# Entry of x: rows scaled before the turn, the turn made with the identity, six PSUM banks, two engines emptying them

## The chip, the cores and the metric

The kernel runs on one core of one Trainium2 chip. The metric is the device time of one execution in microseconds (us). The engines are TensorE (PE in the rows), VectorE (DVE), ScalarE (ACT), GpSimd (POOL) and SyncE (SP), which here only issues transfers.

## The reference, cut to what matters

One layer of a hybrid network on 512 tokens of width 2048. Everything begins with a normalised x that is multiplied by a wide weight matrix:

```python
def rms_norm(x, g):
    xf = x.astype(jnp.float32)
    y = xf * lax.rsqrt(jnp.mean(xf * xf, axis=-1, keepdims=True) + NORM_EPS)
    return (y * g.astype(jnp.float32)).astype(x.dtype)

h = rms_norm(x, norm_mix[l])
proj = h @ w_in[l]
u_s5, x_lru, g_lru, p_rw, z_ssd, xbc_ssd, dt_ssd = _split(proj, [...])
```

Four mixers (an S5 scan, an RG-LRU, an RWKV-7 recurrence, an SSD block) then work on the columns of `proj`, an output projection adds to x, and a mixture of 64 experts follows, then a last norm.

## The kernel before, in words

All data are fp32. The program is one stream of instructions for each engine, in an order written out by hand, with semaphores between them.

**The entry**, which the change touches, goes from x in memory to `hT`, the normalised x with its 2048 channels on the partitions (16 chunks of 128 channels, 512 tokens wide). The tokens come in four tiles `i` of 128 rows (`NTT` is 4), `xs[:, i, :]` of 128x2048.

- SyncE loads the four tiles (L515), then the first slab of w_in (L528), then 18 small parameter tables (L508), then the second slab of w_in.
- ScalarE loads six small tables, then squares each tile and sums its rows (L898), and takes the root of the mean (L900), which it tells by `rs_ok`. Behind the fourth tile its queue issues the S5 tables and others (L901 to L918), and only then comes its first exponential for the S5 parameters (L928).
- VectorE inverts the root (L1212), 128x1, and writes a diagonal matrix from it: the identity times the factor, 128x128 (`rdiag`, L1214, told by `setup_ok`).
- TensorE first turns the table with the norm's gains (L2079; VectorE copies it to `colB`, L1218), then makes one ordinary matmul for every 128x128 block of x against the diagonal (L2088). That turns the block and scales it at once. Four blocks `j` fill one PSUM bank; bank number `m` runs over 16 groups, group `m` being tile `m // 4` and channel chunks `4 * (m % 4)` on. Four banks (2 to 5) are used in turn, so group m waits until group m - 4 has been emptied (`tr_used`).
- VectorE empties every group with one product with the gains, 128x512 (L1226).
- TensorE then begins the projection (L2284): 38 column tiles `n`, each 16 matmuls of 128x128 by 128x512. An ordinary fp32 matmul stands as two MATMUL records in the trace, a transpose as one. Behind column tile 0 it turns the S5 tables (L2093, L2096), for which they must have landed. ScalarE copies each column tile to SBUF (L925).

GpSimd meanwhile zeroes buffers (L671 to L687, the last two of 128x2048 for the S5 matrices), writes the ones of the identity (L689, told by `mask_ok`) and builds masks (L692 to L717).

## Time and profile before

| | |
|---|---|
| median of 3 runs | 2533.95 us (2529.70, 2533.95, 2533.98) |
| profiled execution, its own time | 2538.04 us |
| its span | 2535.9 us |
| mean granted TensorE clock | 0.968 |
| entry: first block of x turned | 10.34 us |
| entry: last group emptied | 28.17 us |
| projection begins | 27.28 us |

The span is what the hardware profiler covers of one execution; some 2 us of the execution's own time lie outside it. All times in the rows below count from the start of the span.

### The profile page before, as it was taken

How to read it: one execution, taken by the hardware profiler on the slowest of the kernel's cores; microseconds unless marked ns; L12 is line 12 of the kernel's file. 1: busy time of each engine (PE TensorE's matmuls, PEld its weight loads, DVE VectorE, ACT ScalarE, POOL GpSimd, SP SyncE). 2: the span in 40 equal slices, each digit the busy share in tenths (PEclk: the TensorE clock that was granted, in tenths of full speed). 3: DMA queues.
4: the chain of work that ended last, by engine and by line, in shares of the span. 5: the costliest groups of instructions: out<-in, count | busy, mean ns of one | idle time of the engine just before them, and what ended most of it. 6: DMA issues, size and time to landing. Idle time of an engine off the chain costs nothing.

```text
span 2535.9 us, 32657 instructions
## 1 busy us (share of the span) xinstructions
PE 2327.9 (92%) x12979; PEld 1218.8 (48%) x12979; DVE 836.9 (33%) x1324; ACT 351.8 (14%) x596; POOL 395.5 (16%) x577
## 2 busy tenths in 40 slices
PE   8999999999899999999998988988888988888886
PEld 5443444455588876644443444444443444344442
DVE  5499937434644432411111111111111111111114
ACT  2100023201422222110000000000000000000002
POOL 3366400000042200011111101111011111111110
PEclk9999999999999999999999999999999999999998
DMA  6221221221122145599999999999999999999998
GB/s 190 69 81 33 67 66 55 67 66 61 42 93 71 49 155 212 220 400 424 426 425 427 425 425 426 426 427 424 426 426 428 426 425 426 427 427 424 425 426 332
DMA packets 143251, 714.61 MB, mean 282 GB/s; under 512 B 33768, under 2 KB 92972, under 8 KB 99788
## 3 DMA queue, kind: packets, MB, share of 16 engines
q1 hardware_dynamic: 115688, 691.09, 66.6%
q0 software_dynamic: 18432, 16.83, 1.9%
q10 hardware_dynamic: 9060, 5.68, 0.8%
q8 instruction: 53, 0.87, 0.1%
q14 instruction: 18, 0.15, 0.0%
HBM read 718.11 MB, written 45.61 MB: 301 GB/s over the span
## 4 chain that ended last, share of the span: by engine, by line
PE 43%; DMA 42%; DVE 11%; issue 2%; ACT 1%; POOL 0%; SPq 0%; DVEq 0%; ACTq 0%; POOLq 0%
DMA big<-in_moe_w 41%; PE ps L2284 12%; PE ps L2631 11%; PE ps L2338 5%; DVE big L1246 4%; PE ps L2660 3%; PE ps L2508 2%; PE ps L2428 1%; DVE big L1378 1%; DVE big L1377 1%; PE ps L2413 1%; PE ps L2645 1%; DMA big<-y_rows 1%; DVE big L1415 1%; PE ps L2088 1%
## 5 line engine op out<-in xcount | busy, mean ns | idle before, releaser
L2631 PE MATMUL ps<-big 128*64 128x384 f32 x4096 | 697.2, 495 | 103.6 <-DMA big<-in_moe_w 90.8
L2631 PEld LDWEIGHTS ps<-big 128*64 128x64 f32 x4096 | 298.5, 139 | 509.2 <-issue 369.9
L2284 PE MATMUL ps<-big 128*128 128x512 f32 (+1 forms) x1184 | 519.1, 598 | 1.6 <-ACT big L946 1.6
L2660 PE MATMUL ps<-big 128*64 128x512 f32 x1536 | 388.8, 661 | 51.7 <-DVE big L2023 51.7
L2284 PEld LDWEIGHTS ps<-big 128*128 128x128 f32 (+1 forms) x1184 | 224.3, 191 | 287.2 <-issue 285.1
L2019 DVE TENSOR_SCALAR big<-ps,scal 128x384 f32<-128x384 f32 x64 | 39.5, 618 | 698.8 <-PE ps L2631 698.8
L2660 PEld LDWEIGHTS ps<-big 128*64 128x64 f32 x1536 | 115.1, 150 | 277.9 <-issue 217.3
L2030 DVE SCALAR_TENSOR_TENSOR big<-ps,scal,big 128x512 f32<-128x512 f32 x128 | 90.2, 747 | 388.6 <-PE ps L2660 388.6
L2338 PE MATMUL ps<-big 128*128 128x256 f32 x768 | 184.8, 391 | 3.6 <-DMA big<-in_w_out 2.5
L2338 PEld LDWEIGHTS ps<-big 128*128 128x128 f32 x768 | 142.3, 192 | 28.7 <-issue 4.8
L846 POOL COPY scal<-slots 128x3 f32 (+1 forms) x64 | 11.9, 186 | 906.8 <-DVE big L2030 888.8
L1180 ACT ACTIVATE big<-ps,scal 128x384 f32<-128x384 f32 x64 | 37.1, 580 | 798.5 <-PE ps L2631 769.4
L2645 PE MATMUL ps<-stacked,big 128*128 128x64 f32 x768 | 141.2, 334 | 0.8 <-issue 0.8
L2645 PEld LDWEIGHTS ps<-stacked,big 128*128 128x128 f32 x768 | 138.8, 261 | 1.4 <-issue 1.4
L1246 DVE TENSOR_TENSOR big<-big 128x512 f32<-128x512 f32 (+7 forms) x129 | 110.8, 880 | 47.1 <-ACT big L953 40.0
L1185 ACT ACTIVATE big<-ps 128x192 f32<-128x192 f32 x64 | 21.1, 330 | 522.4 <-PE ps L2645 522.4
L1945 DVE TENSOR_TENSOR big<-ps,gffn 128x512 f32<-128x512 f32 x128 | 82.5, 686 | 0.5
L925 ACT ACTIVATE big<-ps 128x512 f32<-128x512 f32 (+2 forms) x38 | 22.5, 594 | 431.8 <-PE ps L2284 431.8
L2615 PEld LDWEIGHTS ps<-ident,big 128*128 128x128 f32 x512 | 62.0, 194 | 38.6 <-issue 38.6
L2615 PE MATMUL ps<-ident,big 128*128 128x128 f32 x512 | 74.1, 288 | 0.8 <-DMA big<-x_rows,idxg 0.8
L842 POOL DMA_INDIRECT big<-x_rows,gix x62 | 64.7, 1043 | 55.6 <-POOL gix L838 52.0
L857 POOL DMA_INDIRECT y_rows<-big,six x63 | 64.1, 1018 | 55.7 <-POOL six L854 55.7
(412 smaller groups left out, 1701.5 us busy)
## 6 DMA issues: line engine op xcount, KB each, us to landing
big<-in_moe_w SPq DMA_DIRECT2D x191, 3072.0 KB, 38.6
big<-in_w_in SPq DMA_DIRECT2D x18, 2048.0 KB, 8.4
big<-in_w_out SPq DMA_DIRECT2D x8, 1024.0 KB, 6.0
big<-y_rows SPq DMA_DIRECT2D x8, 1024.0 KB, 11.8
big<-in_x SPq DMA_DIRECT2D x4, 1024.0 KB, 8.4
big<-in_w_out SPq DMA_DIRECT2D x8, 512.0 KB, 7.5
big<-in_x SPq DMA_DIRECT2D x16, 256.0 KB, 2.8
big<-in_w_out SPq DMA_DIRECT2D x1, 4096.0 KB, 15.8
```

Of the source, the lines that this page charges most:

```text
L842: nc.gpsimd.indirect_dma_start(xg[k], None, x2g, bass.IndirectOffsetOnAxis(ap=of, axis=0), bounds_check=T * GR - 1, oob_is_err=False).then ...
L857: nc.gpsimd.indirect_dma_start(ydg, bass.IndirectOffsetOnAxis(ap=six[k][:, 0:1], axis=0), yb[k], None, bounds_check=2 * T * GR - 1, oob_is ...
L1246: v.do(nc.vector.tensor_tensor(out, a, b, o))
L1945: nc.vector.tensor_tensor(xT[k][:, cs, :].rearrange("p c (g t) -> p c g t", g=GR), ps[h][:, 0:NJ * P // 2].rearrange("p (c g t) -> p c g t ...
L2030: nc.vector.scalar_tensor_tensor(out=yb[k][:, cs], in0=ps[5 + q][:], scalar=scal[k][:, 0:1], in1=yb[k][:, cs], op0=MUL, op1=ADD).then_inc( ...
L2284: last = nc.tensor.matmul(ps[n % 2][0:wd, :], ring[s % 2][:, k, c:c + wd], hT[:, k, :], start=(k == 0), stop=(k == NC - 1))
L2338: last = nc.tensor.matmul(ps[b][:, 256 * i:256 * i + 256], ready[c][:, P * (2 * h + i):P * (2 * h + i) + P], w, start=(j == 0), stop=(j == ...
L2508: last = nc.tensor.matmul(o[:], V_[:, q, P * i:P * i + P], wo_rw[:, q, 512 * ncol:512 * ncol + 512], start=(q == 0), stop=(q == WT - 1))
L2615: last = nc.tensor.transpose(ps[h][:, P * j:P * j + P], xg[k].rearrange("t (p c) -> t c p", c=NJ)[:, c], ident[:])
L2631: last = nc.tensor.matmul(ps[2 + w][B * g:B * g + B, 0:FF], xT[k][:, j, B * g:B * g + B], W13[k][w][:, NJ * g + j, :], start=(j == 0), sto ...
L2645: last = nc.tensor.matmul(o, uv[k][:, w, :].rearrange("p (t c) -> p c t", c=FC)[:, m], stacked[:], start=True, stop=True)
L2660: last = nc.tensor.matmul(ps[5 + q][B * g:B * g + B, :], hid[k][:, m, :], W2[k][:, m, 512 * n:512 * n + 512], start=(m == 0), stop=(m == F ...
```

## The change

The rows of x are scaled before they are turned. For tiles 0, 1 and 2 GpSimd multiplies the 128x2048 tile in place by the factor that VectorE has inverted (told by `xsc_ok`), tile 3 is multiplied by VectorE itself. TensorE then turns the blocks in transpose mode with the plain identity. The groups use six banks in turn (2, 3, 4, 5, 7, 1) in place of four. VectorE empties the groups of tiles 0, 1 and 3; those of tile 2 (m = 8 to 11) are emptied by ScalarE, with one 128x128 copy with a scale for each block, sixteen in all, told by `tr_used_act`. The identity is finished before the large memsets on GpSimd; the last large memset (`Gin[1]`) comes behind the three multiplications.

```diff
-        rdiag = big[:, 76, :]
...
+        xsc_ok = sem("xsc_ok")
+        XBANK = (2, 3, 4, 5, 7, 1)
...
             nc.gpsimd.memset(prmB, 0.0).then_inc(zero_ok, 1)
+            g.settle()
+            nc.gpsimd.affine_select(out=ident[:], in_=ident[:], compare_op=ALU.not_equal, fill=1.0, base=0,
+                                    pattern=[[-1, P]], channel_multiplier=1).then_inc(mask_ok, 1)
...
             nc.gpsimd.memset(Gin[0], 0.0)
+
+            for i in range(NTT - 1):
+                pool.wait_ge(setup_ok, i + 1)
+                nc.gpsimd.tensor_scalar(xs[:, i, :], xs[:, i, :], st[:, 8 + i:9 + i], None, ALU.mult).then_inc(xsc_ok, 1)
             nc.gpsimd.memset(Gin[1], 0.0).then_inc(gin_zero, 1)
-            pool.wait_ge(gin_zero, 1)
-            nc.gpsimd.affine_select(out=ident[:], in_=ident[:], compare_op=ALU.not_equal, fill=1.0, base=0,
-                                    pattern=[[-1, P]], channel_multiplier=1).then_inc(mask_ok, 1)
+            pool.wait_ge(gin_zero, GIN_ZERO + 1)
...
                 nc.scalar.activation(st[:, 4 + i:5 + i], st[:, i:i + 1], ACT.Sqrt, bias=epsb[:], scale=1.0 / D).then_inc(rs_ok, 1)
+            act.wait_ge(prm_col, 1)
+            for c4 in range(4):
+                m = 4 * (NTT - 2) + c4
+                act.wait_ge(tr_ok, m + 1)
+                for j in range(4):
+                    c = 4 * c4 + j
+                    g0 = PB["norm_mix"][0] + c
+                    last = nc.scalar.activation(hT[:, c, P * (NTT - 2):P * (NTT - 1)], ps[XBANK[m % 6]][:, P * j:P * j + P], ACT.Copy,
+                                                scale=colB[:, g0:g0 + 1])
+                last.then_inc(tr_used_act, 1)
...
-            def rms_diag(i):
+            def rms_factor(i):
                 dve.wait_ge(rs_ok, i + 1)
-                v.do(nc.vector.reciprocal(st[:, 8 + i:9 + i], st[:, 4 + i:5 + i]))
-                v.settle()
-                v.tell(nc.vector.tensor_scalar(rdiag[:, P * i:P * i + P], ident[:], st[:, 8 + i:9 + i], None, ALU.mult), setup_ok, i + 1)
-
-            rms_diag(0)
+                ins = nc.vector.reciprocal(st[:, 8 + i:9 + i], st[:, 4 + i:5 + i])
+                if i < NTT - 1:
+                    v.tell(ins, setup_ok, i + 1)
+                else:
+                    v.do(ins)
+                    v.settle()
+                    v.tell(nc.vector.tensor_scalar(xs[:, i, :], xs[:, i, :], st[:, 8 + i:9 + i], None, ALU.mult), setup_ok, i + 1)
+
+            rms_factor(0)
...
+            rms_factor(1)
-            for m in range(NTT * 4):
+            for m in [m for m in range(NTT * 4) if m // 4 != NTT - 2]:
                 i, c4 = divmod(m, 4)
-                if c4 == 2 and i + 1 < NTT:
-                    rms_diag(i + 1)
+                if c4 == 2 and i < 2:
+                    rms_factor(i + 2)
...
                 if c4 == 0:
-                    pe.wait_ge(setup_ok, i + 1)
-                if m >= 4:
-                    pe.wait_ge(tr_used, m - 3)
+                    if i < NTT - 1:
+                        pe.wait_ge(xsc_ok, i + 1)
+                    else:
+                        pe.wait_ge(setup_ok, i + 1)
+                if m >= 6:
+                    turned_out(m - 6)
                 for j in range(4):
                     c = 4 * c4 + j
-                    last = nc.tensor.matmul(ps[2 + m % 4][:, P * j:P * (j + 1)], xs[:, i, P * c:P * (c + 1)], rdiag[:, P * i:P * i + P],
-                                            start=True, stop=True)
+                    last = nc.tensor.transpose(ps[XBANK[m % 6]][:, P * j:P * (j + 1)], xs[:, i, P * c:P * (c + 1)], ident[:])
...
                     if n == 0 and k % 4 == 0:
-                        pe.wait_ge(tr_used, NTT * 4 - 3 + k // 4)
+                        for i in (NTT - 2, NTT - 1):
+                            turned_out(4 * i + k // 4)
```

`turned_out(m)` waits on TensorE until group m has been emptied, by ScalarE's count for tile 2 and by VectorE's for the others.

On VectorE, at the start of its stream, the order before (`st` holds the norm factors, `ps` is a PSUM bank, `big` is SBUF: the diagonal in the row with `ident`, `hT` in the rows with `colB`):

```order
L1212 RECIPROCAL st<-st 128x1
L1214 TENSOR_SCALAR big<-ident,st 128x128
L1218 COPY colB<-ps 128x128
L1226 TENSOR_TENSOR big<-ps,colB 128x4x128 x2
L1212 RECIPROCAL st<-st 128x1
L1214 TENSOR_SCALAR big<-ident,st 128x128
L1226 TENSOR_TENSOR big<-ps,colB 128x4x128 x4
L1212 RECIPROCAL st<-st 128x1
L1214 TENSOR_SCALAR big<-ident,st 128x128
L1226 TENSOR_TENSOR big<-ps,colB 128x4x128 x4
L1212 RECIPROCAL st<-st 128x1
L1214 TENSOR_SCALAR big<-ident,st 128x128
```

and of the change (the row `big<-big,st` is the multiplication of tile 3 in place):

```order
L1228 RECIPROCAL st<-st 128x1
L1238 COPY colB<-ps 128x128
L1228 RECIPROCAL st<-st 128x1
L1247 TENSOR_TENSOR big<-ps,colB 128x4x128 x2
L1228 RECIPROCAL st<-st 128x1
L1247 TENSOR_TENSOR big<-ps,colB 128x4x128 x4
L1228 RECIPROCAL st<-st 128x1
L1234 TENSOR_SCALAR big<-big,st 128x2048
L1247 TENSOR_TENSOR big<-ps,colB 128x4x128 x6
```

The four small diagonals are gone, one multiplication of 128x2048 stands between the emptying of m = 5 and m = 6, and 12 groups are left of 16.

On GpSimd, from the small memsets on, before (`big` is the parameter tables, then the LRU, S5 and the two `Gin` buffers):

```order
L679 MEMSET big 128x1024
L680 MEMSET eps 128x1
L681 ISA
L681 IOTA tk 128x32
L683 IOTA tk 128x16
L685 MEMSET big 128x1024
L686 MEMSET big 128x2048
L687 MEMSET big 128x2048
L689 AFFINE_SELECT ident<-ident 128x128
L692 MEMSET tri 128x128
```

and of the change (the row `big<-big,st` is the multiplication of tiles 0 to 2):

```order
L681 AFFINE_SELECT ident<-ident 128x128
L683 MEMSET big 128x1024
L684 MEMSET eps 128x1
L685 IOTA tk 128x32
L687 IOTA tk 128x16
L689 MEMSET big 128x1024
L690 MEMSET big 128x2048
L694 TENSOR_SCALAR big<-big,st 128x2048 x3
L695 MEMSET big 128x2048
L698 MEMSET tri 128x128
```

The identity has moved ahead of 6 rows, and the three multiplications stand ahead of the last large memset and of all masks.

On ScalarE, behind the last squared tile, before:

```order
L898 ACTIVATE big,st<-big 128x2048
L900 ACTIVATE st<-st,epsb 128x1
L901 DMA ldt<-in_s_log_dt 16x2
L902 DMA big<-in_s_lambda_re 16x128
L903 DMA big<-in_s_lambda_im 16x128
```

and of the change:

```order
L904 ACTIVATE big,st<-big 128x2048
L906 ACTIVATE st<-st,epsb 128x1
L914 ACTIVATE big<-ps,colB 128x128 x16
L917 DMA ldt<-in_s_log_dt 16x2
L918 DMA big<-in_s_lambda_re 16x128
```

Sixteen copies from PSUM now stand ahead of all the transfers that ScalarE issues here.

## Rows read from the trace of the kernel before

**Rows 1.** The page: the chain that ended last, its shares of the span by line

```profile
DMA big<-in_moe_w 41%; PE ps L2284 12%; PE ps L2631 11%; PE ps L2338 5%; DVE big L1246 4%; PE ps L2660 3%; PE ps L2508 2%; PE ps L2428 1%; DVE big L1378 1%; DVE big L1377 1%; PE ps L2413 1%; PE ps L2645 1%; DMA big<-y_rows 1%; DVE big L1415 1%; PE ps L2088 1%
```

**Rows 2.** The chain in order of time: start us, us, what

```profile
4.18 5.79 DMA big<-in_rw_mu
...
10.54 16.90 PE ps L2088 x128
27.44 13.74 PE ps L2284 x32
```

**Rows 3.** Timeline of the entry: start us, us, engine line op out<-in [idle before]

```profile
5.38 1.79 POOL L687 MEMSET big<- 128x2048 f32 x1
...
8.02 0.29 ACT L900 ACTIVATE st<-st,epsb 128x1 f32<-128x1 f32 x1
...
10.58 0.29 DVE L1218 COPY colB<-ps 128x128 f32<-128x128 f32 x1 [1.62 <-PE ps L2079]
10.78 0.29 ACT L900 ACTIVATE st<-st,epsb 128x1 f32<-128x1 f32 x1
...
12.36 0.69 DVE L1226 TENSOR_TENSOR big<-ps,colB 128x512 f32<-128x512 f32 x1 [1.49 <-PE ps L2088]
...
13.12 0.29 ACT L900 ACTIVATE st<-st,epsb 128x1 f32<-128x1 f32 x1
...
15.67 0.29 ACT L900 ACTIVATE st<-st,epsb 128x1 f32<-128x1 f32 x1
```

**Rows 4.** Windows, L2088 alone: us, PE busy (records), PEld, granted clock, DMA, GB/s

```profile
12.30:14.30 2.00, 2.00 (x11) 2.00 (x11) 1.00 1.01 349
16.00:18.00 2.00, 2.00 (x20) 2.00 (x19) 1.00 1.10 349
```

**Rows 5.** Timeline of TensorE, transposes alone

```profile
82.71 3.66 PE L2104 MATMUL ps<-ident,big 128*128 128x128 f32 x32
...
693.88 1.06 PE L2381 MATMUL ps<-ident,big 128*128 128x128 f32 x4
```

**Rows 6.** Groups of GpSimd and VectorE: count | busy us, mean ns | idle

```profile
L714 POOL TENSOR_TENSOR tris<-tri,ident 128x128 f32<-128x128 f32 x1 | 0.5, 452 | 0.1
...
L741 POOL TENSOR_TENSOR big<-big 128x512 f32<-128x512 f32 x16 | 16.7, 1042 | 0.0
...
L748 POOL TENSOR_TENSOR big<-big 128x512 f32<-128x512 f32 x16 | 31.4, 1961 | 1.3
...
L1250 DVE TENSOR_SCALAR big<-big 128x2048 f32<-128x2048 f32 x1 | 1.2, 1227 | 0.4 <-ACT big L970 0.4
```

**Rows 7.** Timeline at 63 us, VectorE beside GpSimd

```profile
63.27 1.04 POOL L741 TENSOR_TENSOR big<-big 128x512 f32<-128x512 f32 x1
63.36 0.97 DVE L1350 SCALAR_TENSOR_TENSOR lsp<-lsp 128x4 f32<-128x4 f32 x1
64.36 0.17 DVE L1250 TENSOR_SCALAR lsp<-lsp 128x4 f32<-128x4 f32 x1
```

**Rows 8.** Groups of ScalarE: a copy from PSUM of 128x192

```profile
L1185 ACT ACTIVATE big<-ps 128x192 f32<-128x192 f32 x64 | 21.1, 330 | 522.4 <-PE ps L2645 522.4
```

**Rows 9.** Issues of L908 (count, ns min/median/max, first and last start), then landing

```profile
L908 ACTq DMA_DIRECT2D big<-in_s_c_im x2: 1074/1426/1779, 27.0 to 28.8; - x2
...
DMA to landing us min/median/max: 3.2/5.2/9.8
```

**Rows 10.** Issues of L528, the slabs of w_in, and landing

```profile
L528 SPq DMA_DIRECT2D big<-in_w_in x19: 367/368/448, 2.9 to 575.2; - x19
...
DMA to landing us min/median/max: 6.2/8.4/16.8
```

**Rows 11.** Windows of TensorE around a stall, and at 695 us: us, busy, granted clock

```profile
190.00:193.00 3.00, 0.00 (x0) 1.00 0.00 0
...
193.50:200.00 6.50, 6.50 (x12) 0.50 0.00 0
...
695.00:696.00 1.00, 1.00 (x12) 0.93 0.00 0
```

More of the change, by code:

```diff
@@ L428, in build @@
         setup_ok, rs_ok = sem("setup_ok"), sem("rs_ok")
-        tr_ok, tr_used = sem("tr_ok"), sem("tr_used")
+        tr_ok, tr_used, tr_used_act = sem("tr_ok"), sem("tr_used"), sem("tr_used_act")
+        xsc_ok = sem("xsc_ok")
+        XBANK = (2, 3, 4, 5, 7, 1)
         prm_tr, prm_col = sem("prm_tr"), sem("prm_col")
-        gin_zero, gin_ok = sem("gin_zero"), sem("gin_ok")
+        gin_zero, GIN_ZERO, gin_ok = zero_ok, 2, sem("gin_ok")
         g_tr, g_got = sem("g_tr"), sem("g_got")
@@ L1226, in _ @@
                 nc.vector.tensor_tensor(
-                    hT[:, 4 * c4:4 * c4 + 4, P * i:P * (i + 1)], ps[2 + m % 4][:].rearrange("p (a n) -> p a n", a=4),
+                    hT[:, 4 * c4:4 * c4 + 4, P * i:P * (i + 1)], ps[XBANK[m % 6]][:].rearrange("p (a n) -> p a n", a=4),
                     colB[:, g0:g0 + 4].to_broadcast([P, 4, P]), ALU.mult).then_inc(tr_used, 1)
@@ L2079, in _, with turned_out @@
             nc.tensor.transpose(ps[6][:, 128:256], prmB, ident[:]).then_inc(prm_tr, 1)
+            def turned_out(m):
+                i, c4 = divmod(m, 4)
+                if i == NTT - 2:
+                    pe.wait_ge(tr_used_act, c4 + 1)
+                else:
+                    pe.wait_ge(tr_used, m + 1 - 4 * (i == NTT - 1))
             for m in range(NTT * 4):
@@ L2082, in _ @@
                 if c4 == 0:
-                    pe.wait_ge(setup_ok, i + 1)
-                if m >= 4:
-                    pe.wait_ge(tr_used, m - 3)
+                    if i < NTT - 1:
+                        pe.wait_ge(xsc_ok, i + 1)
+                    else:
+                        pe.wait_ge(setup_ok, i + 1)
+                if m >= 6:
+                    turned_out(m - 6)
                 for j in range(4):
                     c = 4 * c4 + j
-                    last = nc.tensor.matmul(ps[2 + m % 4][:, P * j:P * (j + 1)], xs[:, i, P * c:P * (c + 1)], rdiag[:, P * i:P * i + P],
-                                            start=True, stop=True)
+                    last = nc.tensor.transpose(ps[XBANK[m % 6]][:, P * j:P * (j + 1)], xs[:, i, P * c:P * (c + 1)], ident[:])
                 last.then_inc(tr_ok, 1)
```

## The prediction

> **What bounds the kernel now.** I read the page first, for what the chain that ended last consists of: transfers of expert weights, then matmuls, L2284 above all, and L2088, the turning of x, with 1% [rows 1]. One per cent of 2536 us is 25, so the whole change plays within the first 28 us. The chain in order of time shows how they hang together: the small tables land at 9.97 us, 128 records of L2088 take 16.90 us without a hole, and the first projection matmuls stand right behind them [rows 2]. So in the entry the bound is TensorE itself, from 10.5 to 27.4 us, and nobody it waits for. The timeline shows who stands beside it: VectorE empties a group in 0.69 us, ScalarE has its four roots at 8.31, 11.07, 13.41 and 15.96 us, and GpSimd is done with all but its last memset at 5.38 us [rows 3].
>
> The pace of L2088 comes from the windows. Between 12.3 and 14.3 us there are 11 records, between 16 and 18 us 20 of them; one at each edge counted off that is some 0.21 and 0.107 us for one [rows 4]. The granted clock reads 1.00 in both rows; the pace says that the first stretch ran at the lower level (1.2 GHz) and the second at 2.4 GHz, and VectorE's first group, emptied at 12.36, fits: 8 records of 0.213 from 10.34 and 0.31 us until it has them [rows 3]. From the count of records the change of level lies near 16 us.
>
> **What the change adds and removes.** 64 ordinary matmuls of two records each become 64 transposes of one record. 32 transposes take 3.66 us at the upper level, the tail of the last among it, so 0.11 us for one [rows 5], the same as a record of L2088. At the lower level four take 1.06 us with their tail [rows 5]; I take the 0.213 of a record of L2088 for one there too. So a group of four is 0.44 us where it was 0.87, or 0.85 where it was 1.7. Turning would take 7 us at the upper level; what decides is now who feeds TensorE and who empties its banks. I follow the groups m.
>
> *Feeding.* The first root is there at 8.31; with 0.3 us for the reciprocal and the hand-over GpSimd starts on tile 0 at 8.6. The trace has no multiplication by a factor on GpSimd. From below stands its memset of the same 128x2048, 1.79 us [rows 3]; from above a product of two tensors, which goes from 0.45 us at 128 to 1.04 at 512 elements [rows 6], 1.54 ns for each further one, so 3.4 us at 2048. I take 2.0, nearer to the memset, since one tensor is read and not two. Tile 0 is then ready at 8.6 + 2.0 = 10.7 (hidden until 10.5 by the tables that TensorE needs first), tile 1 at 11.3 + 2.0 = 13.4, tile 2 (root at 13.41, VectorE's reciprocal at 13.6) at 15.7. With the lower level until 16 us TensorE starts m = 0 at 10.8 and m = 4 at 14.2: tiles 1 and 2 come in time and cost nothing.
>
> *Emptying.* VectorE has m = 4 at 15.3 and m = 5 at 16.2, and is done with it at 16.9. Now comes the new piece in its queue: the reciprocal of tile 3 and its multiplication, 1.23 us by the row of 128x2048 [rows 6], so from 17.05 to 18.3. It may be held up: a VectorE operation on 128x4 elements took 0.97 us while a GpSimd product ran and ended with it, where its like takes 0.17 [rows 7]. GpSimd's last memset of 1.79 us now begins at 15.7 and ends at 17.5, so at worst the multiplication starts at 17.5. I take the middle, done at 18.6. Behind it wait m = 6 and m = 7, and for their banks wait m = 12 and m = 13 of TensorE: two groups of 0.69 give 20.0. TensorE, at the upper level by then, has turned m = 6 to 12 in the meantime. Then m = 13, 14 and 15 at 0.44 are done at **21.4 us**, and the projection starts, since m = 12 is emptied at about 20.7. It needs m = 15 only 10 us later, behind 12 of its matmuls.
>
> *ScalarE* gets m = 8 at 17.4. A copy of 128x192 took 0.33 us [rows 8]; sixteen at most as long are 5.3 us, so it is done between 20.6 and 22.7. TensorE's m = 14 and 15 need only its first two groups. Its first slab of w_in also has to be there: issued at 2.9 us, it is the one that took 16.8 us [rows 10], so it lands at 19.7 and hides below 21.4; that is also the floor of any gain.
>
> *Sum.* The first projection record began at 27.3 us, the same moment to 0.15 us as in the chain [rows 2]; 27.3 - 21.4 = **5.9 us** saved. Everything behind the projection's start waits for its column tiles and moves as one block: the slabs wait for them, the S5 chain on VectorE starts only after column tiles, and so on to the expert weights. The masks on GpSimd come some 10 us later, and nobody asks for them before the slabs are through. The span was 2535.9 and that execution's own time 2538.04; the median is 2533.95, 4.1 us lower. I take the saving off the median: **2528.1 us**, 0.23% faster. About 0.2%, 5.1 us, is what a measurement of this kernel can tell from no change, and the three runs themselves lie 4.3 us apart.
>
> *A rule against it.* Of the transposes the clock shows this: it stood low beside those of L2381 at 693.9 us and rose within the microsecond from 695 [rows 5, 11], so transposes did not keep it low. The Trainium skill says otherwise (TensorE: Matmul & The Clock Gate, Part 4: PE-mode transpose): in transpose mode the full clock "doesn't engage", as it isn't counted as busy in the same way. By that rule the sum would be the first rival below, by the row it is the one above.
>
> *A second one.* For the multiplication on GpSimd the Trainium skill has a price (GPSIMD Reference, section 3.1): about 1.8 cycles at 1.2 GHz for an element in a tight loop, an estimate of 3.1 us for 2048. By it tile 2 would be ready at 17.9 and the sum would end near 21.6. No run here shows that operation yet.
>
> **The rivals.**
>
> *The clock stays low through the transposes.* 64 at 0.213 are 13.6 us, from 10.8 to 24.4; then the projection begins at the lower level. After the stall at 190 us TensorE worked 6.5 us at 0.50 before it rose [rows 11]; the same here is 3.25 us lost, 27.7 in all: 0.4 us worse, **2534.3**. For it: the start of the entry is at the lower level anyway, and transposes in number appear in the trace only at the upper one. Against it: the row at 695. Chance 8%.
>
> *GpSimd is slow, like its two-input products.* At 3.4 us a tile, tile 2 is ready at 8.6 + 10.2 = 18.8, and eight groups at 0.44 bring 22.4: 4.9 us saved, **2529.1**. Chance 12%.
>
> *GpSimd loses its SBUF access to VectorE.* The same form of product takes 1.04 us in L741 and 1.96 us on average in L748 [rows 6]. Four times 1.96 is 7.8 us a tile: tile 2 at 32.0, the end at 35.5, 8.3 us lost: **2542.2**. This turns the sign where a tile takes more than (27.3 - 3.5 - 8.6) / 3 = 5.1 us. Against it: VectorE's products here read one operand from PSUM, and it idles half of the time. Chance 5%.
>
> *The S5 tables come late.* ScalarE issues them behind its sixteen copies, from 21.2 us instead of 15.7. The last was issued at 28.8 and landed 3.2 us later, at 32.0 [rows 9], 16.3 us after the first issue. If that distance holds they land at 37.5, but TensorE wants them behind column tile 0, at 21.4 + 13.74 = 35.2 [rows 2]: a wait of 2.3 us, 3.6 saved, **2530.3**. For it: the queue's order. Against it: it was the first slabs that made those issues slow, and they would be nearly through. Chance 10%.
>
> *The gain is lost further down*, in other stalls or clock levels there, 2532 to 2534. Chance 5%.
>
> **How the numbers follow.** The forecast has 60%: 2528.1, with 21.0 to 22.2 for the projection's start by the unknown costs. Its 5.9 us stand just beyond 5.1, so I give three quarters of it to faster (45%); with a part of slow GpSimd and of the S5 tables that makes 52%. Slower: the 5% of GpSimd without access. The rest, 43%, is within 0.2%. For the range, the low end is the forecast less the 4.3 us of scatter, 2523.8; the high end takes in the clock's rival, 2534.4.
>
> **What would show it.** Right: one record for each block, 0.21 us apart before some 16 us and 0.11 after; GpSimd's three rows of 2.0 us; VectorE's 128x2048 row between 17 and 18.8 us; the first projection record at 21.4, and no idle time ahead of L2126/L2129. Wrong: a GpSimd row above 3.4 us, transposes at 0.21 us beyond 20 us, projection records 0.85 us apart, or TensorE idle at 35 us for a transfer.

## The result, and the profile after

The change makes the kernel slower: 2538.32 us (median of 20 runs, 2534.71 to 2542.38) against 2533.55 (20 runs, 2529.70 to 2537.74), a ratio of 1.0023 with a 95% interval of 1.0016 to 1.0029. By the medians that is 4.8 us more. The forecast was 2528.1, 5.9 us less than before.

| | before | change |
|---|---|---|
| profiled execution, its own time | 2538.04 us | 2537.32 us |
| its span | 2535.9 us | 2535.3 us |
| first block of x turned | 10.34 us | 14.27 us |
| projection begins | 27.28 us | 30.52 us |

The profiled execution of before took longer than any of its 20 runs (4.5 us over their median) and that of the change lay 1.0 us under its own median, so the spans can't be set against each other; the entry can. The chain of waits of the change, in order of time, where before had one unbroken row of L2088 [rows 2] (start us, us, what):

```profile
8.77 10.89 POOL big L694 x2
...
19.70 0.67 PE ps L2121 x4
...
20.40 1.29 DVE big L1247 x2
...
21.79 6.12 DVE big L1234
27.91 0.60 DVE big L1247
...
28.65 2.04 PE ps L2121 x16
30.69 13.74 PE ps L2318 x32
44.42 0.11 PE ps L2126
```

Before, the entry was TensorE's own work. Now it is 10.9 us of GpSimd and 6.1 us of one VectorE instruction; only 2.7 us of the chain are transposes. The groups of the change between 5 and 45 us (count | busy us, mean ns of one | idle time before it, and what ended it):

```profile
L694 POOL TENSOR_SCALAR big<-big,st 128x2048 f32<-128x2048 f32 x3 | 16.3, 5442 | 3.1 <-DVE st L1228 3.1
...
L2121 PE MATMUL ps<-ident,big 128*128 128x128 f32 x64 | 10.9, 341 | 9.5 <-POOL big L694 9.3 <-DVE big L1247 0.2
...
L1247 DVE TENSOR_TENSOR big<-ps,colB 128x512 f32<-128x512 f32 x12 | 7.8, 685 | 6.3 <-PE ps L2121 6.1
...
L1234 DVE TENSOR_SCALAR big<-big,st 128x2048 f32<-128x2048 f32 x1 | 6.1, 6123 | 0.0
L914 ACT ACTIVATE big<-ps,colB 128x128 f32<-128x128 f32 x16 | 4.2, 418 | 10.3 <-PE ps L2121 10.3
```

One GpSimd multiplication takes 5.44 us. TensorE stands idle for 9.5 us in L2121, and GpSimd ended 9.3 us of it, three waits in all. The timeline of the change gives the places:

```profile
14.27 3.57 PE L2121 MATMUL ps<-ident,big 128*128 128x128 f32 x16 [3.98 <-POOL big L694]
...
19.70 1.97 PE L2121 MATMUL ps<-ident,big 128*128 128x128 f32 x16 [1.85 <-POOL big L694]
...
25.03 1.80 POOL L695 MEMSET big<- 128x2048 f32 x1
...
25.13 3.27 PE L2121 MATMUL ps<-ident,big 128*128 128x128 f32 x16 [3.46 <-POOL big L694]
26.35 2.44 ACT L914 ACTIVATE big<-ps,colB 128x128 f32<-128x128 f32 x9 [10.28 <-PE ps L2121]
26.89 1.16 POOL L698 MEMSET tri<- 128x128 f32 x1
27.83 1.27 DVE L1247 TENSOR_TENSOR big<-ps,colB 128x512 f32<-128x512 f32 x2
28.00 0.20 POOL L699 MEMSET rmask<- 64x128 f32 x1
```

The tiles come at 14.2, 19.6 and 25.1 us, a strict 5.4 us apart. VectorE begins its multiplication of tile 3 at 21.79 us, while the third GpSimd multiplication runs, and ends at 27.91, which is 1.08 us after the large memset has ended (25.03 + 1.80 = 26.83). Meanwhile the next memset, L698, takes 1.16 us where its like, L699, takes 0.20. The granted clock is the third thing that is new (windows of TensorE of the change: us, busy (records), granted clock, DMA share, GB/s):

```profile
22.00:24.00 2.00, 0.00 (x0) 1.00 1.07 350
24.00:26.00 2.00, 0.87 (x4) 0.61 1.07 359
26.00:28.00 2.00, 2.00 (x12) 0.54 0.31 100
28.00:30.00 2.00, 1.75 (x16) 1.00 0.02 2
```

The third wait for GpSimd is 3.46 us long, from 21.67 to 25.13. The granted clock falls within it, before a transpose of tile 2 has run: by half microseconds it reads 0.94 from 24.0 and 0.50 from 24.5 us. TensorE then works at the lower level (1.2 GHz) until some 27.9 us. Tile 0's sixteen transposes were slow too, 3.57 us for tile 1's 1.97, though the column reads 1.00 there; their pace is that of the lower level, as it is in the entry of the kernel before.

### The profile page after: what moved, and what is told of

Its sections match the earlier page's. It is cut to its first block, busy times and chain, and to the rows that moved or that the text cites. A ratio compares the mean times of both kernels' runs of the same rounds, so it can differ in the third digit from the quotient of the medians.

```text
span 2535.3 us, 32544 instructions
## 1 busy us (share of the span) xinstructions
PE 2322.2 (92%) x12915; PEld 1212.0 (48%) x12915; DVE 838.7 (33%) x1317; ACT 356.4 (14%) x612; POOL 413.6 (16%) x580
## 4 chain that ended last, share of the span: by engine, by line
PE 45%; DMA 39%; DVE 12%; issue 2%; ACT 1%; POOL 1%; SPq 0%; ACTq 0%; DVEq 0%; POOLq 0%
DMA big<-in_moe_w 38%; PE ps L2318 12%; PE ps L2665 12%; PE ps L2372 5%; DVE big L1267 4%; PE ps L2694 4%; PE ps L2542 2%; PE ps L2462 1%; DVE big L1399 1%; PE ps L2679 1%; DVE big L1398 1%; PE ps L2447 1%; DMA big<-y_rows 1%; PE ps L2649 1%; DVE big L1436 1%
## 5 line engine op out<-in xcount | busy, mean ns | idle before, releaser
L2372 PEld LDWEIGHTS ps<-big 128*128 128x128 f32 x768 | 142.1, 191 | 27.3 <-issue 4.8
```

The costliest lines, as they stand in the source:

```text
L2372: last = nc.tensor.matmul(ps[b][:, 256 * i:256 * i + 256], ready[c][:, P * (2 * h + i):P * (2 * h + i) + P], w, start=(j == 0), stop=(j == ...
```

## The experiments

The experiments were made to separate four things: what a GpSimd multiplication costs and why, what holds VectorE's multiplication, what the clock adds, and whether the time follows the projection's start at all. Each ratio is to the kernel before on the same chip, with its 95% interval, which is some 2 us to either side; differences in us are those of the medians.

### The form of the multiplication on GpSimd

```diff
-            for i in range(NTT - 1):
-                pool.wait_ge(setup_ok, i + 1)
-                nc.gpsimd.tensor_scalar(xs[:, i, :], xs[:, i, :], st[:, 8 + i:9 + i], None, ALU.mult).then_inc(xsc_ok, 1)
+            pool.wait_ge(setup_ok, 1)
+            nc.gpsimd.tensor_scalar(xs[:, 0, 0:1024], xs[:, 0, 0:1024], st[:, 8:9], None, ALU.mult)
+            nc.gpsimd.tensor_scalar(xs[:, 0, 1024:], xs[:, 0, 1024:], st[:, 8:9], None, ALU.mult).then_inc(xsc_ok, 1)
+            pool.wait_ge(setup_ok, 2)
+            nc.gpsimd.tensor_scalar(xs[:, 1, :], xs[:, 1, :], 1.0, None, ALU.mult).then_inc(xsc_ok, 1)
+            pool.wait_ge(setup_ok, 3)
+            nc.gpsimd.tensor_tensor(xs[:, 2, :], xs[:, 2, :], st[:, 10:11].to_broadcast([P, D]), ALU.mult).then_inc(xsc_ok, 1)
```

> GpSimd took 5.44 us for each multiplication of 128x2048 by the factor. This kernel gives it three other forms: tile 0 the same operation in two halves of 1024, tile 1 a multiplication by the constant 1.0 (the factor of tile 1 is left out), tile 2 a product of two tensors with the factor broadcast. Theory A, the price is that of any pass of GpSimd over 2048 fp32 elements in place: halves of 2.7 us, the constant 5.4 us, the product of two tensors at least 5.4 us. Theory B, the price is the pointer to a scalar: halves of 2.7 us, the constant near the memset's 1.8 to 2.0 us, the product 3.4 us, as its smaller shapes in the trace of before have it.

One run, 2537.4 us, beside 2533.48 for the kernel before. The timeline of GpSimd in it:

```profile
8.66 2.85 POOL L693 TENSOR_SCALAR big<-big,st 128x1024 f32<-128x1024 f32 x1 [2.98 <-DVE st L1232]
11.50 2.83 POOL L694 TENSOR_SCALAR big<-big,st 128x1024 f32<-128x1024 f32 x1
14.32 5.36 POOL L696 TENSOR_SCALAR big<-big 128x2048 f32<-128x2048 f32 x1
19.66 3.59 POOL L698 TENSOR_TENSOR big<-big,st 128x2048 f32<-128x2048 f32 x1
```

Half the size takes 2.85 us, so the cost is by element (2.7 ns) and not by instruction. A constant in place of the factor takes 5.36, so the factor read from SBUF is not it. The product of two tensors takes 3.59 us, two thirds of the form that reads one tensor. So each theory was right in one part and wrong in another: the constant costs as much as the factor (A), and the product of two tensors is the cheaper form (B). Why the form that reads one tensor is the slower one, no run shows. Nor is the cost VectorE's doing: in the change the tile 0 multiplication ran from 8.8 to 14.2 us, while VectorE had a copy of 0.29 and a reciprocal of 0.16 us to do, and took as long as the next, with five VectorE operations beside it.

### The product of two tensors for all three tiles

```diff
-                nc.gpsimd.tensor_scalar(xs[:, i, :], xs[:, i, :], st[:, 8 + i:9 + i], None, ALU.mult).then_inc(xsc_ok, 1)
+                nc.gpsimd.tensor_tensor(xs[:, i, :], xs[:, i, :], st[:, 8 + i:9 + i].to_broadcast([P, D]), ALU.mult).then_inc(xsc_ok, 1)
```

> One edit to the change: GpSimd scales its three tiles by a product of two tensors, the factor broadcast, which took 3.59 us for 128x2048 where the multiplication by a scalar took 5.44. Theory: GpSimd's three operations set the entry. They end at 8.8 + 10.8 = 19.6 us, the memset behind them at 21.4, VectorE's multiplication of tile 3 at 22.6 at the latest, m = 6 and 7 at 24.0, the projection starts at 25.4 us, 1.9 us ahead of the kernel before, and the time is 1.9 us below it. Rival: VectorE's evictions and GpSimd's products slow each other down (two operands on each); then the products take over 4.5 us and the projection starts after 27.3 us.

Measured 2533.62 us, 0.9997 (0.9988 to 1.0006): of the change's 4.8 us over the kernel before 0.4 are left, by another form of the same product on GpSimd. The projection starts at 24.78 us, 2.5 before the kernel before and 0.6 before what was expected; the time does not show those 2.5, so it misses the expected 1.9 below. The timeline:

```profile
8.62 10.71 POOL L694 TENSOR_TENSOR big<-big,st 128x2048 f32<-128x2048 f32 x3 [2.95 <-DVE st L1228]
...
17.91 4.25 DVE L1234 TENSOR_SCALAR big<-big,st 128x2048 f32<-128x2048 f32 x1
...
19.27 1.81 POOL L695 MEMSET big<- 128x2048 f32 x1
...
21.14 1.16 POOL L698 MEMSET tri<- 128x128 f32 x1
```

VectorE is held here too, and again it ends (22.16) 1.08 us after the memset (21.08).

### All four tiles scaled on VectorE

GpSimd scales nothing, and its masks wait until tile 3 is scaled.

```diff
-            for i in range(NTT - 1):
-                pool.wait_ge(setup_ok, i + 1)
-                nc.gpsimd.tensor_scalar(xs[:, i, :], xs[:, i, :], st[:, 8 + i:9 + i], None, ALU.mult).then_inc(xsc_ok, 1)
             nc.gpsimd.memset(Gin[1], 0.0).then_inc(gin_zero, 1)
...
+            pool.wait_ge(setup_ok, NTT)
             nc.gpsimd.memset(tri[:], 1.0)
...
-                if i < NTT - 1:
-                    v.tell(ins, setup_ok, i + 1)
-                else:
-                    v.do(ins)
-                    v.settle()
-                    v.tell(nc.vector.tensor_scalar(xs[:, i, :], xs[:, i, :], st[:, 8 + i:9 + i], None, ALU.mult), setup_ok, i + 1)
+                v.do(ins)
+                v.settle()
+                v.tell(nc.vector.tensor_scalar(xs[:, i, :], xs[:, i, :], st[:, 8 + i:9 + i], None, ALU.mult), setup_ok, i + 1)
...
+            dve.wait_ge(zero_ok, 3)
...
-                    if i < NTT - 1:
-                        pe.wait_ge(xsc_ok, i + 1)
-                    else:
-                        pe.wait_ge(setup_ok, i + 1)
+                    pe.wait_ge(setup_ok, i + 1)
```

The added wait on VectorE stands far behind the entry, ahead of its first S5 phases, until GpSimd's memsets are done; the kernels below in which GpSimd scales nothing or its masks wait have it too.

> All four tiles are scaled by VectorE, GpSimd's masks wait until that is done; transposes, six banks and ScalarE's share stay. Theory: feeding by GpSimd is the whole loss. VectorE's multiplications take 1.23 to 1.29 us each, tile 0 is ready at 9.9 us, the projection starts at 22.4 us instead of 27.3 before, and the time is 4.9 us below the kernel before. Rival 1: TensorE stays at its lower level through the transposes, the projection starts at 24 to 25 us and its first records stand 0.85 us apart, 0 to 2 us below before. Rival 2: something behind the entry (S5 tables, the expert weights) takes the gain back: the projection starts at 22 to 23 us and the time is that of before.

Measured 2529.2 us, 0.9983 (0.9974 to 0.9992). It is 4.3 us faster than the kernel before, near the 4.9 expected, and the only version here whose interval lies clearly below that kernel's time. TensorE's timeline:

```profile
10.28 8.17 PE L2114 MATMUL ps<-ident,big 128*128 128x128 f32 x48
19.87 2.04 PE L2114 MATMUL ps<-ident,big 128*128 128x128 f32 x16 [1.42 <-DVE big L1242]
21.75 6.60 PE L2311 MATMUL ps<-big 128*128 128x512 f32 x15
```

and its windows for the transposes alone:

```profile
12.00:14.00 2.00, 2.00 (x11) 1.00 0.99 358
14.00:15.00 1.00, 1.00 (x7) 1.00 1.10 348
...
16.00:18.00 2.00, 2.00 (x19) 1.00 1.10 348
```

So the halved work of TensorE is real: 16 transposes in 2.0 us. TensorE's level rose beside nothing but transposes, near 15.5 us by their pace (11 records in 2 us before, 19 after; the column reads 1.00 throughout), as it had in the kernel before near 16. The same run with GpSimd's masks not waiting:

```diff
-            pool.wait_ge(setup_ok, NTT)
             nc.gpsimd.memset(tri[:], 1.0)
```

> The version that scales on VectorE alone, without the wait that kept GpSimd's masks behind it, so that GpSimd works on its masks from 7.5 to 18 us, beside the multiplications. Theory: a VectorE multiplication between SBUF operands is held while GpSimd works, memsets among it. Then tiles 0 to 3 take over 1.29 us each, some 0.3 to 1.0 us more, and the projection starts at 22.5 to 25 us instead of 21.8. Rival: only large or two-operand work of GpSimd holds it; then all four take 1.29 us and the start stays at 21.8 us.

Measured 2530.66 us, 0.999 (0.9981 to 1.0). The four multiplications take 1.31, 1.57, 1.43 and 1.47 us in place of 1.28 to 1.29, and the projection starts at 22.30. Beside short GpSimd operations a multiplication loses 0.03 to 0.29 us; beside the long ones it loses whole microseconds.

### The scaling undone, the six banks and ScalarE's share kept

```diff
-                    last = nc.tensor.transpose(ps[XBANK[m % 6]][:, P * j:P * (j + 1)], xs[:, i, P * c:P * (c + 1)], ident[:])
+                    last = nc.tensor.matmul(ps[XBANK[m % 6]][:, P * j:P * (j + 1)], xs[:, i, P * c:P * (c + 1)], rdiag[:, P * i:P * i + P],
+                                            start=True, stop=True)
```

with the diagonals of the kernel before, and nothing scaled on GpSimd.

> The scaling alone is undone: the diagonal and ordinary matmuls are back, with six banks and ScalarE emptying tile 2. Theory: the entry before was bound by TensorE's records, so banks and a second engine bring nothing: the projection starts at 27.3 us to within 0.5, the time is that of before to within 1.5 us. Rival: part of the loss of the change comes from ScalarE's copies and its later transfers; then this kernel is slower than before by 1 to 3 us too.

Measured 2532.3 us, 0.9995 (0.9985 to 1.0004), projection at 26.91, both as expected. Banks and ScalarE's sixteen copies by themselves neither gain nor cost more than the interval lets show.

### What holds VectorE's multiplication

First the last large memset moved behind the masks:

```diff
-            nc.gpsimd.memset(Gin[1], 0.0).then_inc(gin_zero, 1)
-            pool.wait_ge(gin_zero, GIN_ZERO + 1)
...
+            nc.gpsimd.memset(Gin[1], 0.0).then_inc(gin_zero, 1)
+            pool.wait_ge(gin_zero, GIN_ZERO + 1)
```

> The last large memset on GpSimd moves behind the masks. Theory: VectorE's multiplication of tile 3 is held as long as GpSimd works on large tiles, first by its third multiplication (to 25.1 us), then by the memset (to 26.8 us). Then it ends at 26.4 us instead of 27.9, the projection starts at about 29.0 instead of 30.5, and the time is about 1.5 us below that of the change. Rival: the multiplication is slow for a reason of its own beside any work on GpSimd; then it ends at 27.9 as before and nothing is gained.

Measured 2538.2 us, 1.0016 (1.0007 to 1.0025): as the change, and the projection starts at 31.34, not at 29.0. The small memsets took the large one's place, as GpSimd's timeline shows:

```profile
25.03 0.20 POOL L696 MEMSET tri<- 128x128 f32 x1
...
25.88 0.10 POOL L700 MEMSET misc<- 128x16 f32 x1
26.06 1.15 POOL L703 TENSOR_SCALAR_AFFINE_SELECT tri<-tri 128x128 f32<-128x128 f32 x1
```

and VectorE's:

```profile
21.87 5.20 DVE L1234 TENSOR_SCALAR big<-big,st 128x2048 f32<-128x2048 f32 x1
```

It ends at 27.07, 1.09 us after the last of the memsets that stand end to end; the affine select behind them has a gap of 0.08 us in front of it, and it is now the one that takes 1.15 us for 0.29. So VectorE is done 0.8 us before its time in the change, and still the projection starts 0.8 us later than there. TensorE shows why, by its timeline and its windows:

```profile
25.12 6.38 PE L2121 MATMUL ps<-ident,big 128*128 128x128 f32 x32 [2.38 <-POOL big L694]
```

```profile
20.00:22.00 2.00, 2.00 (x14) 0.60 0.74 184
...
28.00:30.00 2.00, 2.00 (x11) 0.50 0.01 0
```

In this execution the granted clock fell near 20.4 us, behind a wait of 2.15 us and with tile 1 under way, and stayed at 0.50 until some 30.6. The 32 transposes of tiles 2 and 3 take 6.4 us, mostly at that level and one behind the other. The clock alone sets the start here. Then the memset and the masks were made to wait for tile 3, here and with the product of two tensors:

```diff
+            pool.wait_ge(setup_ok, NTT)
             nc.gpsimd.memset(Gin[1], 0.0).then_inc(gin_zero, 1)
```

> The change, with GpSimd's last large memset and all masks held until VectorE has scaled tile 3. Theory A (only operations that run on GpSimd at the same time hold VectorE's multiplication, and the holder is whatever runs): it starts at 21.8 us, is held by the third GpSimd multiplication to 25.1, and is done at 25.1 to 26.4, in place of 27.9; the projection starts at 27.7 to 29.0 in place of 30.5. If the time follows the projection's start one for one, 1.5 to 2.8 us less than the change, 2535.5 to 2536.8. Theory B (the multiplication takes 6.1 us whenever it has begun beside a GpSimd multiplication, whatever follows): done at 27.9, projection at 30.5, time as the change, 2538.3.

> As the run before in this call, but with the product of two tensors on GpSimd (3.57 us a tile). Theory A: VectorE's multiplication starts at 17.9 us and is done at 19.4 to 20.6 in place of 22.2, the projection starts at 22.6 to 23.3. If the time follows the projection's start one for one from the kernel before (27.3 us and 2533.4), 2529.0 +- 1.2. The rival is that kernels with the new entry carry some 2 us of their own (the form with the product of two tensors started 2.5 us before the kernel before and took as long): 2531.2.

Here the memset and the masks wait, so nothing of GpSimd stands behind its third multiplication. The first kernel took 2538.64 us, 1.002 (1.0011 to 1.0029), the second 2531.11, 0.9992 (0.9983 to 1.0001). Their VectorE rows, of the first:

```profile
22.39 3.65 DVE L1235 TENSOR_SCALAR big<-big,st 128x2048 f32<-128x2048 f32 x1
```

and of the second:

```profile
18.66 1.92 DVE L1235 TENSOR_SCALAR big<-big,st 128x2048 f32<-128x2048 f32 x1
```

They end at 26.04 and 20.58, which is 1.08 us after the third GpSimd multiplication (24.96 and 19.50) in both. So theory A held for VectorE, whose multiplication ends with the last GpSimd operation that stands without a gap, whatever that is. The 1.08 us are most of the 1.29 that it takes undisturbed, so that nearly all of it seems to be done behind the gap. Where GpSimd went on at once (the change, two tensors, memset late) its next operation took 1.15 to 1.16 us and was held in its turn. The second kernel's projection starts at 23.2, near the expected 22.6 to 23.3, but its time is that of the rival, 2531.2, some 2 us more than the start alone would give. The first one misses theory A on both counts, since its start hardly moves: 30.23 us. Its start and time are those of theory B, whose mechanism the VectorE row rules out. Its TensorE timeline says why:

```profile
25.02 5.38 PE L2123 MATMUL ps<-ident,big 128*128 128x128 f32 x32 [2.02 <-POOL big L694]
```

Its windows around that:

```profile
23.00:25.00 2.00, 0.00 (x0) 1.00 1.09 377
25.00:27.00 2.00, 1.98 (x14) 0.75 1.03 325
27.00:29.00 2.00, 2.00 (x11) 0.50 0.04 12
```

32 transposes at mostly the lower level take 5.4 us where they take 3.8 at the upper, as the second kernel has them, behind a wait of 0.85 us:

```profile
19.56 3.81 PE L2123 MATMUL ps<-ident,big 128*128 128x128 f32 x32 [0.85 <-POOL big L694]
```

With VectorE's hold gone, the clock stands in its place.

### The clock

Matmuls of ones in TensorE's waits keep it busy (and with it its clock up):

```diff
+            pe.wait_ge(zero_ok, 1)
+            for _ in range(22):
+                nc.tensor.matmul(ps[0][:, 0:P], ones[:], ones[:], start=True, stop=True)
...
                 if c4 == 0:
+                    for _ in range((14, 14, 14, 5)[i]):
+                        nc.tensor.matmul(ps[0][:, 0:P], ones[:], ones[:], start=True, stop=True)
```

> The change, with matmuls of ones on TensorE wherever it waits in the entry: 22 from 1.7 us on, 14 ahead of each of tiles 0, 1 and 2, and 5 ahead of tile 3, into a bank nobody reads. The entry of the change lost 3.3 us in its profile, its median 4.8 us. Theory: the rest is TensorE's clock, which falls while it waits for GpSimd and is back at a moment that differs from run to run; in this kernel the granted clock is 1.00 from before 12 us up to the projection, the projection starts at 30.3 to 30.6 us, and the time is 3.0 to 3.5 us above the kernel before and so 1 to 2 us below the change. Rival: the rest comes from later parts (S5 tables, masks, expert weights); then the time is that of the change, 4.8 us above before.

Measured 2537.95 us, 1.0019 (1.001 to 1.0028), the projection at 30.46. Tile 0's sixteen transposes now take 1.97 us in place of 3.57, and nothing is gained, since VectorE's 6.13 us lie over it. The time is that of the rival, 4.8 us over the kernel before, and not the 3.0 to 3.5 of the theory: the clock in the entry is not what makes 4.8 out of 3.2. Both together:

```diff
+            for _ in range(22):
+                nc.tensor.matmul(ps[0][:, 0:P], ones[:], ones[:], start=True, stop=True)
...
+            pool.wait_ge(setup_ok, NTT)
             nc.gpsimd.memset(Gin[1], 0.0).then_inc(gin_zero, 1)
```

> The change with both: matmuls of ones in TensorE's waits, and GpSimd's last large memset and masks held until VectorE has scaled tile 3. Theory A (two things stand side by side behind the third GpSimd multiplication, VectorE's multiplication and a low TensorE clock, and each alone covers the other): tile 2 is turned from 25.05 to 26.9 us at the full clock, VectorE's multiplication is done at 26.0, the projection starts at 28.6 in place of 30.5, which is 8.7 + 3 x 5.44 + 3.5. Theory B (something else holds the start at 30.5): no move. The time, by the line through the other kernels: about 1.7 us under the change, 2536.4 +- 1.5.

Measured 2537.51 us, 1.0013 (1.0004 to 1.0022), the projection at 29.85 and not at 28.6. Its TensorE timeline:

```profile
25.18 1.97 PE L2128 MATMUL ps<-ident,big 128*128 128x128 f32 x16 [0.33 <-POOL big L694]
26.98 1.28 PE L2119 MATMUL ps<-ones 128*128 128x128 f32 x10
28.10 1.91 PE L2128 MATMUL ps<-ident,big 128*128 128x128 f32 x16
```

Tile 2 is through at the upper level by 27.2 us and VectorE is done at 26.21, so both holds are gone; but the five matmuls of ones that I had put before tile 3 now stood in the way themselves, for 1.1 to 1.3 us. Less those, the start is 28.6 to 28.7, as expected. A run without the five was not made, so this rests on a subtraction. The kernel with two tensors and waiting masks supports it: it has both holds away and no matmuls of ones, and its projection starts 3.70 us behind the end of the third GpSimd multiplication (23.20 for 19.50). Here that multiplication ends at 25.13, which would give 28.8.

### Does the time follow the projection's start?

The product form began 2.5 us early and gained nothing, and the change cost 4.8 us for 3.2. So the start was moved in the kernel before, without the change. Earlier, by warming TensorE:

```diff
+            pe.wait_ge(zero_ok, 1)
+            for _ in range(22):
+                nc.tensor.matmul(ps[0][:, 0:P], ones[:], ones[:], start=True, stop=True)
             pe.wait_ge(mask_ok, 1)
```

> The kernel before with nothing of the change, and 22 matmuls of ones on TensorE from 1.7 us on, ahead of its first real work. Theory: the entry before is bound by TensorE's 128 records, of which some 27 ran at the lower level and lost 0.107 us each. With the clock up before 10 us the turning takes 13.8 us instead of 16.9, the projection starts at 24.2 us, and the time is 2.5 to 3.1 us below before. Rival: once the records are faster VectorE's emptying or the slab of w_in (19.7 us) is the bound; then less than 1 us is gained.

Measured 2534.81 us, 1.0008 (0.9999 to 1.0017), with the projection at 24.36 as expected, and nothing gained in the time where 2.5 to 3.1 us were expected. And later, by two more squares on ScalarE:

```diff
+            act.wait_ge(x_io[0], 16)
+            nc.scalar.activation(wide(88), xs[:, 0, :], ACT.Square, accum_out=st[:, 41:42]).then_inc(late, 1)
+            act.wait_ge(late, 1)
+            nc.scalar.activation(wide(88)[:, 0:D // 2], xs[:, 0, 0:D // 2], ACT.Square, accum_out=st[:, 42:43]).then_inc(late, 1)
+            act.wait_ge(late, 2)
             for i in range(NTT):
                 act.wait_ge(x_io[i], 16)
```

> The kernel before, with its first root held up by two more squares of tile 0 on ScalarE (3.2 us), results unused. The first block is turned at 13.5 in place of 10.3 us and the projection starts at 30.5, the moment of the change. If the time follows the projection's start one for one, 3.2 us over the kernel before, 2536.6 +- 1.2. If the change carries a further 1.5 us that the entry does not explain, this run shows only the 3.2; if a delay of this size costs more than itself, this run takes 2538.3 too.

Measured 2537.52 us, 1.0015 (1.0006 to 1.0024). Its projection starts at 29.45 in the profile, only 2.2 us late (VectorE had the root 3.2 us late, but the first block came only 1.9 us late, at 12.20, since before it had waited for the tables and not for the root), and it costs 4.4. That is twice its delay, but its interval reaches from 1.5 to 6.1 us and takes in the 2.2, so it isn't shown that a delay of the unchanged kernel costs more than itself, and the three cases of the expectation aren't told apart. All kernels with a median of ten runs or more, by their start (each start is from one profile, and the difference is to the median of the kernel before on the same chip):

| kernel | projection begins, less 27.28 | time, less before |
|---|---|---|
| all on VectorE | -5.5 | -4.3 |
| the same, masks not waiting | -5.0 | -2.5 |
| two tensors, masks waiting | -4.1 | -2.0 |
| before, TensorE warmed | -2.9 | +1.6 |
| two tensors | -2.5 | +0.4 |
| diagonals, six banks | -0.4 | -1.2 |
| before, first root late | +2.2 | +4.4 |
| change, both holds away | +2.6 | +3.8 |
| change, masks waiting | +3.0 | +5.5 |
| change, TensorE busy | +3.2 | +4.8 |
| the change | +3.2 | +4.8 |
| change, memset late | +4.1 | +4.7 |

A line through these and the kernel before (at 0, 0) has a slope of 0.89 us per us (standard error 0.11) and passes 1.7 us above the kernel before; the points scatter about it by 1.3 us, with the warmed kernel 2.5 above and the diagonals 2.5 below. So the time does follow the start, nearly one for one, and the change lies on that line (0.2 us off). What is odd is not the new entry but the kernel before: of a line with that slope drawn through it, eleven of the twelve lie above, by 0.6 to 4.2 us, the two with its own entry among them. Why is open. In single executions the shift of the start is carried to the first record of the output projection, but not exactly beyond (first records in the profiles, us):

| | before | change | before, warmed | all on VectorE |
|---|---|---|---|---|
| projection | 27.3 | 30.5 | 24.4 | 21.8 |
| output projection (L2338 before) | 654.7 | 658.0 | 651.8 | 649.5 |
| expert matmuls (L2631 before) | 1064.0 | 1065.5 | 1060.5 | 1056.6 |
| end of the span | 2535.9 | 2535.3 | 2535.6 | 2526.7 |

In all fourteen profiles, those of every kernel here, the output projection begins 627.4 to 627.8 us behind the projection. From there to the expert matmuls it is 405.0 to 409.3 us, and from there to the end of the span 1469.8 to 1475.1. So the start is carried on exactly for the first 650 us, and what comes on top of it arises behind that point; the kernel before has the longest of the middle stretches, in the one profile of it. Whether its median has the same cause is not shown. Between 1040 and 1070 us TensorE waits and works at lower clock levels at places that differ from execution to execution, for instance in the windows of the kernel before:

```profile
1050.00:1054.00 4.00, 4.00 (x44) 0.52 0.97 378
1054.00:1058.00 4.00, 4.00 (x19) 0.63 0.98 415
```

and of the change:

```profile
1050.00:1054.00 4.00, 3.15 (x19) 0.73 0.99 421
1054.00:1058.00 4.00, 4.00 (x49) 0.84 1.03 442
```

One profile a kernel can't tell a cause there from scatter, and no experiment was made on it.

## Why the prediction was wrong, point by point

*The step that failed* is the first term of the feeding: "I take 2.0, nearer to the memset, since one tensor is read and not two". It measured 5.44 us, and both bounds failed with it, since the upper one, "from above a product of two tensors ... so 3.4 us at 2048", bounds only its own form. That form measured 3.57 to 3.60, so the extrapolation from [rows 6] was good to 6%. The assumption that the form with one tensor is no slower than the one with two had no row behind it, and it carried the sign: tile 2 came at 25.1 us in place of 15.7. By the prediction's own sum that alone moves the start of the projection from 21.4 to 28.5 us; the rest, up to the measured 30.5, is the next step.

*The Trainium skill's price.* What the Trainium skill (GPSIMD Engine Reference, section 3.1) gives with 1.8 cycles for an element is the best case of a tight loop. The estimate of 3.1 us from it was nearer than mine, and still 2.3 us short of the 5.44 measured. For the product of two tensors the same section has about 2.6 cycles and 4.5 us for an add of 2048 fp32 elements, a row that the prediction did not use; here that form took 3.57 to 3.60 us.

*The hold of VectorE's multiplication* was seen from [rows 7], and of its two values the worse was the true one: "at worst the multiplication starts at 17.5", at the end of the memset behind tile 2. The prediction took "the middle". Measured, the multiplication ended 1.08 us behind that memset, close to the 1.23 of the worst case, but the memset now ended at 26.83. Begun at 21.79, it was held for the rest of the third GpSimd multiplication and the whole memset, 6.12 us in place of 1.29. With 5.44 us a tile, the formula of the third rival, which has no term for this hold, gives 8.7 + 16.3 + 3.5 = 28.5 us for the projection; 30.5 was measured. The 2.0 us between are the hold and the low clock side by side, for each alone covers the other, and with both removed the start was 29.85 less the 1.1 to 1.3 of my filler.

*The clock.* "TensorE, at the upper level by then" did not hold in the change for tile 2, whose transposes began at the lower level at 25.13 us. The rival of the low clock had a false mechanism: transposes did not keep it low (48 of them in one row with all on VectorE, with the pace going from 11 to 19 in 2 us beside them). The Trainium skill (TensorE: Matmul & The Clock Gate, Part 4: PE-mode transpose) has the rule that the full clock does not engage in transpose mode; no run here bears it out. What lowered the clock was the idle time in front of the transposes, 3.46 us in the change: with that time filled by matmuls of ones it stayed up. This cost nothing in the change, where VectorE's hold lay over it, some 1.5 us with the memset and masks waiting, and it set the start with the memset late.

*The slower rival* named the right threshold, 5.1 us a tile, and the wrong cause: GpSimd did not lose its access to VectorE. Its rate was the same with VectorE idle; it was VectorE that lost. The rival's price of 7.8 us a tile and its 2542.2 were too high. A chance of 5% for everything beyond 5.1 was too low, since nothing in the trace showed this form on GpSimd.

*Right:* one record for each block, at 0.21 us before the clock rises and 0.11 after (16 in 1.96 to 2.04 us with their tail); VectorE's multiplication at 1.28 to 1.29 us when undisturbed; the groups emptied in 0.69, or 0.60 to 0.65 back to back; ScalarE's sixteen copies, 4.2 us against at most 5.3; and the S5 tables. ScalarE issued them from 28.5 to 34.5 us in the change, and TensorE's transpose of them at 44.26 stands without a wait behind column tile 0, so that rival did not happen. In the kernel with all on VectorE tile 3 was scaled at 19.1 us where the forecast had 18.6, and the projection began at 21.75 where it had 21.4: the sum from there on was sound.

*The sum of the time.* "5.9 us saved" became 3.2 us lost at the projection's start. "Everything behind the projection's start ... moves as one block" holds to 0.4 us up to the output projection, and as a slope of 0.89 for the whole. It does not hold as a difference to the kernel before, which is off that line by 1.7 us; by the line even the forecast start would have gained 3.6 us and not 5.9. The forecast range ended at 2534.4.

## What to carry to other kernels

Before work moves to GpSimd, find a row of the same form on it, not merely of the same size: here the multiplication by one factor cost half again as much as the product of two tensors, and more than four times VectorE's 1.29 us. Long GpSimd operations that stand end to end also held a long VectorE operation on SBUF until the first gap, so a critical one should find GpSimd waiting, and moving the culprit merely names the next one in its queue. Judge a gain of a few microseconds at the front of a long kernel by several variants and a line through them, since one pair can be off by up to 2.5 us here.

## What the runs showed of the hardware that was not expected

- GpSimd's TENSOR_SCALAR on fp32 takes 5.44 us for 128x2048 and 2.85 for 128x1024, with a factor from SBUF or a constant (5.36); TENSOR_TENSOR of 128x2048 takes 3.57 to 3.60, and a memset 1.80.
- VectorE's TENSOR_SCALAR of 128x2048 begun beside GpSimd work ended 1.08 us after the last GpSimd operation before a gap, whether that was a memset or a multiplication: at 27.91 for 26.83, 26.04 for 24.96, 22.16 for 21.08, 20.58 for 19.50. Its products that read PSUM took 0.69 us beside GpSimd's multiplications, as without them.
- GpSimd is held in return: 1.16 us for a memset of 0.20, and 1.15 for an affine select of 0.29.
- In the change TensorE's granted clock fell to its lower level, 0.50, within an idle stretch of 3.46 us, and the sixteen transposes behind it took 3.27 us. With the memset late it fell near 20.4 us, behind a wait of 2.15. In the kernel with all tiles on VectorE, behind a wait of 1.42 us, sixteen transposes took 2.04 us, the upper level's pace. An idle TensorE can cost twice, for the wait and for the pace behind it.
